# Value products of the second attention in split fp32r, heads in pairs, the residual kept in DRAM meanwhile

## What is computed

```python
h = rms_norm_2(x, norm_mix)
proj = h @ w_in                      # q, 3 pairs of k and v, gates, pool input, merge gates
a = nsa_attention(...) @ w_branch_attn
b = pool_mixer(u_pool, pool_w, pool_scale) @ w_branch_pool
ga, gb = jnp.split(jax.nn.sigmoid(g_merge), 2, axis=-1)
x = x + (ga * a + gb * b) @ w_out
h = rms_norm_2(x, norm_mlp)
return x + jnp.square(jax.nn.relu(h @ w_ff1)) @ w_ff2
```

```python
e = jnp.exp(s - jnp.max(s, axis=-1, keepdims=True)) * mask
p = e / jnp.maximum(jnp.sum(e, axis=-1, keepdims=True), 1e-30)
o = g[0] * o_cmp + g[1] * o_sel + g[2] * o_win
```

## Time and profile before

| | us |
|---|---|
| median of 3 runs | 1099.92 |
| lowest and highest run | 1099.74, 1104.56 |
| the profiled execution | 1103.73 |
| its span, first to last instruction | 1101.9 |

### The profile page before, as it was taken

The page is one execution under the profiler, slowest core; times in us unless marked ns, Lnnn a source line. Parts: engine busy times, 40 slices in busy tenths (PEclk is TensorE's granted clock), DMA queues, the critical chain, the costliest instruction groups (busy, mean ns, idle before and its releaser), DMA issues. The chain is left out here.

```text
span 1101.9 us, 14350 instructions
## 1 busy us (share of the span) xinstructions
PE 1078.1 (98%) x5666; PEld 889.8 (81%) x5666; DVE 562.1 (51%) x1076; ACT 449.4 (41%) x814; POOL 80.2 (7%) x90
## 2 busy tenths in 40 slices
PE   7999999999899999999999999999999999999997
PEld 5788877888788888878788888888888888888885
DVE  5578997666864236233666878352222223333334
ACT  7454345545542432353433543233333333222223
POOL 0022110003400007200000000000000000000000
PEclk9999999999999999998999999999999999999999
DMA  8554332125120473131100611243322232224002
GB/s 314 111 114 106 97 95 77 41 61 188 49 87 1 139 223 86 39 90 46 38 1 1 211 44 56 73 153 118 131 77 77 83 147 77 77 77 144 10 1 76
DMA packets 73649, 100.09 MB, mean 91 GB/s; under 512 B 3776, under 2 KB 41408, under 8 KB 73584
## 3 DMA queue, kind: packets, MB, share of 16 engines
q1 hardware_dynamic: 72800, 96.43, 27.1%
q0 software_dynamic: 784, 2.75, 1.7%
HBM read 96.42 MB, written 2.75 MB: 90 GB/s over the span
## 5 line engine op out<-in xcount | busy, mean ns | idle before, releaser
L2036 DVE TENSOR_TENSOR w_lo<-wring,w_hi 128x1024 fp32r<-128x1024 f32 x64 | 78.5, 1226 | 238.1 <-ACT w_hi L1524 238.1
L1524 ACT ACTIVATE w_hi<-wring 128x1024 fp32r<-128x1024 f32 x64 | 67.7, 1058 | 211.5 <-PE bank L736 211.5
L736 PE MATMUL bank<-u_hi,h_hi 128*128 128x512 f32 (+1 forms) x288 | 110.9, 385 | 1.0 <-ACT x L1227 0.8
L736 PE MATMUL bank<-u_hi,h_lo 128*128 128x512 f32 (+1 forms) x288 | 109.2, 379 | 0.0
L736 PE MATMUL bank<-u_lo,h_hi 128*128 128x512 f32 (+1 forms) x288 | 109.0, 378 | 0.0
L1609 DVE TENSOR_TENSOR u_lo<-wring,u_hi 128x1024 fp32r<-128x1024 f32 (+1 forms) x64 | 78.8, 1240 | 53.9 <-ACT u_hi L1309 53.3
L736 PE MATMUL bank<-h_hi,w_lo 128*128 128x512 f32 (+2 forms) x272 | 104.5, 384 | 0.0
L736 PE MATMUL bank<-h_hi,w_hi 128*128 128x512 f32 (+2 forms) x272 | 104.4, 384 | 0.0
L736 PE MATMUL bank<-h_lo,w_hi 128*128 128x512 f32 (+2 forms) x272 | 104.3, 384 | 0.0
L736 PE MATMUL bank<-w_lo,ff_hi 128*128 128x512 f32 x256 | 101.0, 395 | 0.0
L1309 ACT ACTIVATE u_hi<-wring 128x1024 fp32r<-128x1024 f32 (+1 forms) x64 | 65.7, 1032 | 86.0 <-PE bank L736 70.1
(11 more groups left out here) (285 smaller groups left out, 2030.0 us busy)
## 6 DMA issues: line engine op xcount, KB each, us to landing
wring<-in_w_ff SPq DMA_DIRECT2D x16, 2048.0 KB, 8.1
wring<-in_w_in SPq DMA_DIRECT2D x60, 512.0 KB, 3.9
arena<-in_w_out SPq DMA_DIRECT2D x4, 1024.0 KB, 5.0
wring<-in_w_out SPq DMA_DIRECT2D x2, 2048.0 KB, 13.2
arena<-in_first SPq DMA_DIRECT2D x8, 418.0 KB, 6.8
arena<-in_x SPq DMA_DIRECT2D x4, 512.0 KB, 10.6
arena<-bias_copies POOLq DMA_DIRECT2D x8, 256.0 KB, 6.3
arena<-bias_copies SPq DMA_DIRECT2D x32, 64.0 KB, 2.2
```

Source lines behind the costliest of these rows:

```text
L736: last = mm(b, lhs, rhs, start=(start and n == 0), stop=(stop and n == 2))
L1524: run(dst, src, ACT.Copy).then_inc(w_hi_done, 1)
L2036: v.tensor_tensor(cut(w_lo[ring3(m)]), src, cut(w_hi[ring3(m)]).bitcast(F32), ALU.subtract).then_inc(w_lo_done, 1)
```

## The change

The value products change roles. `v2_both` holds, for each branch, tile and group, 64 columns of high half and 64 of low half side by side, 128 weights wide. The moving operand is the transposed probabilities of two heads of one group, 256 columns, once as `pt_hi` and once as `pt_lo`. The result is the attention transposed, with the high half's rows 0 to 63 and the low half's 64 to 127 of a bank; ACT copies the low rows to SBUF (`low_rows`) and DVE adds them per head (`collect2`) into `attnT`, which is kept transposed.

Since the rows of the result are no longer the query rows, the scaling by gate over sum moves ahead of the transposes: DVE takes the reciprocal of two sums, and POOL multiplies each probability row by it and by the gate. Both branches then accumulate in one bank. `steps2` is ordered tile, head pair, branch, head. There are six `logits2` buffers, and transposes run two passes behind the scores, values three. ACT takes the high half of the transposed probabilities, DVE the low one.

The compression branch is scaled before its transposes too, and its four products give `attnT` at once. The attention transposes go. Branch products 0 and 1 move up behind the transposes of the last two pairs. The fills are spread over steps 0 to 52.

`v2_both` and the `pt` halves need room, part of which is where `x` lies: SP writes `x` to DRAM among the loads of the second block, and reads it back when the last value product is done.

```diff
-    steps2 = [(i, br, h) for i in range(NT) for br in ("s", "w") for h in range(NH)]
+    steps2 = [(i, br, 2 * m + r) for i in range(NT) for m in range(NH // 2) for br in ("s", "w") for r in range(2)]
...
-    fill2 = [(m, FILL2[m // KC], m % KC) for m in range(KC * len(FILL2))]
+    fill2 = [(m * 9 // 8, FILL2[m // KC], m % KC) for m in range(KC * len(FILL2))]
...
-    BRANCH_HIGH = {56: 0, 59: 1}
+    BRANCH_HIGH = {58: 0, 62: 1}
...
-    AT_STEP = {50: 0, 54: 1, 58: 2}
+    AT_STEP = {56: 0, 58: 1, 60: 2}
...
+                        if U2 + 5 <= u < U2 + 9:
+                            i = u - U2 - 5
+                            sp.wait_ge(xn_done, i + 1)
+                            sp.dma_start(x_kept[i], x[:, i, :]).then_inc(x_out, 16)
...
                 if name == "w2o1":
+                    sp.wait_ge(pv_done, 2 * NS)
+                    sp.wait_ge(x_out, 16 * NT)
+                    for i in range(NT):
+                        sp.dma_start(x[:, i, :], x_kept[i]).then_inc(x_back, 16)
                     for e in range(3, KC):
                         load_branch(e)
...
             def turn2(u):
-                pe.wait_ge(e_done, NS + u + 1)
+                pe.wait_ge(scaled, u + 1)
...
+            def value2(t):
+                i, br, h = steps2[t]
+                o, at, n = t // NH, t % NH // 4 * 256, t // 2 % 2
+                pe.wait_ge(t_free, TT[("pt", NS + t + 1)] + 1)
...
                 for j in range(i + 1):
+                    for part in (pt_hi, pt_lo):
+                        last = mm(bank[6 + o % 2][:, at:at + 256], v2_both[:, "sw".index(br), j, h // GROUP, :, :].rearrange("p m d -> p (m d)"),
+                                  part[n][:, 256 * j:256 * (j + 1)], start=(br == "s" and j == 0 and part is pt_hi),
+                                  stop=(br == "w" and j == i and part is pt_lo))
+                last.then_inc(pv_done, 2)
...
+            pe.wait_ge(v2_lo_done, 2)
+            for t in range(0, NS + 6, 2):
                 if t < NS:
                     pe.wait_ge(l_done, NS + t)
                     pair2(t)
                     fill(fill2, t)
                     fill(fill2, t + 1)
+                if 4 <= t < NS + 4:
+                    turn2(t - 4)
+                    turn2(t - 3)
+                if t >= 6:
+                    value2(t - 6)
+                if t == NS:
+                    pe.wait_ge(a_free, A2_END)
+                    pe.wait_ge(pm_lo_done, 4)
+                if t in (NS, NS + 2):
+                    branch_product((t - NS) // 2)
...
+            for t in range(0, NS + 8, 2):
+                if t < NS:
+                    exps(t, steps2, NS, den2, logits2)
+                if 4 <= t < NS + 4:
+                    prob_high(t - 4)
+                    prob_high(t - 3)
+                if t < NS:
+                    exps(t + 1, steps2, NS, den2, logits2)
+                if t >= 14 and t % NH == 6:
+                    low_rows((t - 14) // NH)
+                if t in AT_STEP:
+                    attn_high(AT_STEP[t])
...
             def collect2(o):
+                i, g = o // G2, o % G2
+                dve.wait_ge(lo_rows_done, o + 1)
...
+                for r in range(2):
+                    v.tensor_tensor(turned[r * HD:(r + 1) * HD, :].rearrange("p (m s) -> p m s", m=2), cut(bank[6 + o % 2][0:HD, :], r),
+                                    cut(lo_rows, r), ALU.add).then_inc((turned_done, o_free)[r], 1)
...
+                place = attnT[:, 2 * g:2 * g + 2, i * P:(i + 1) * P]
+                v.tensor_tensor(place, place, turned.rearrange("p (m s) -> p m s", m=2), ALU.add).then_inc(attn_done, 1)
...
+            for t in range(0, NS + 8, 2):
+                if t < NS:
+                    score2(t)
+                if 2 <= t < NS + 2:
+                    dve.wait_ge(e_done, NS + t)
+                    v.reciprocal(den2[:, t - 2:t], den2[:, t - 2:t]).then_inc(rden_done, 1)
+                if t < NS:
+                    score2(t + 1)
+                if 4 <= t < NS + 4:
+                    prob_low(t - 4)
+                    prob_low(t - 3)
+                if t >= 14 and t % NH == 6:
+                    collect2((t - 14) // NH)
                 if t - 2 in AT_STEP:
                     attn_low(AT_STEP[t - 2])
...
+            for u, (i, br, h) in enumerate(steps2):
+                if u % 2 == 0:
+                    pool.wait_ge(rden_done, u // 2 + 1)
+                place = logits2[u % 6][:, 0:(i + 1) * P]
+                at = (NH if br == "s" else 2 * NH) + h
+                g.tensor_scalar(place, place, den2[:, u:u + 1], gates[:, i, at:at + 1], ALU.mult, ALU.mult).then_inc(scaled, 1)
```

More of the change, by code:

```diff
@@ L252, in build @@
         x = sb("x", [P, NT, D])
+        x_at = nc.sbuf_base - 4 * NT * D
         hT_at = nc.sbuf_base
@@ L1103, in _ @@
-            for t in range(0, NS + 4, 2):
+                    for part in (pt_hi, pt_lo):
[3 more added lines that the diff above has]
+                last.then_inc(pv_done, 2)
+            R = 2 * NT
@@ new lines, in branch_product @@
+            def branch_product(at):
+                e, n = BRANCH[at]
+                pe.wait_ge(br_lo_done, e + 1)
+                if at >= 4:
+                    pe.wait_ge(r_free, 2 * NT + at - 3)
+                act = (a_hi, a_lo) if n == 0 else (pm_hi, pm_lo)
+                for k in range(4):
+                    last = three(bank[(2 * NT + at) % 4][:, :], (br_hi[e % 2], br_lo[e % 3]), slice((4 * n + k) * P, (4 * n + k + 1) * P),
+                                 act, slice(k * S, (k + 1) * S), True, k == 0, k == 3)
+                last.then_inc(r_full, 1)
@@ L1460, in _ @@
                         split_high(m)
+                    act.wait_ge(x_out, 16 * NT)
+                    for n, br in enumerate("sw"):
+                        act.wait_ge(a_free, AT[("kv2" if br == "s" else "kwvg", NT - 1)] + 1)
+                        run(v2_both[:, n, :, :, 0, :], v2[br].rearrange("p i (g d) -> p i g d", g=G2), ACT.Copy).then_inc(v2_hi_done, 1)
                 if kind == "hidk":
@@ new lines, in prob_high @@
+            def prob_high(u):
+                n, r = u // 2 % 2, u % 2
+                k = TT[("pt", NS + u)]
+                blocks = steps2[u][0] + 1
+                act.wait_ge(t_full, k + 1)
+                if u >= 4:
+                    act.wait_ge(pv_done, NS + 2 * (u // 2) - 2)
+                run(pt_hi[n][:, :].rearrange("p (j r s) -> p j r s", r=2, s=P)[:, 0:blocks, r, :],
+                    bank[4 + k % 2][:, 0:blocks * P].rearrange("p (j s) -> p j s", s=P), ACT.Copy).then_inc(pt_hi_done, 1)
@@ new lines, in low_rows @@
+            def low_rows(o):
+                act.wait_ge(pv_done, NS + NH * (o + 1))
+                if o >= 1:
+                    act.wait_ge(o_free, NS // NH + o)
+                run(lo_rows, bank[6 + o % 2][HD:P, :], ACT.Copy).then_inc(lo_rows_done, 1)
+            act.wait_ge(pooled, len(POOL_WINDOWS))
+            act.wait_ge(v2_lo_done, 2)
+            for t in range(0, NS + 8, 2):
[10 more added lines that the diff above has]
+                    attn_high(AT_STEP[t])
+                for u in (t, t + 1):
+                    takes(fill2, u)
+                    if u in GB_HIGH:
+                        high(GB_HIGH[u])
+                    if u in BRANCH_HIGH:
+                        branch_high(BRANCH_HIGH[u])
@@ L1953, in collect2, with prob_low @@
-            def collect2(o):
-                i = steps2[NH * o][0]
-                dve.wait_ge(o_free, NS // NH + o + 1)
-                ins = v.tensor_tensor(attn[:, i, :], attn[:, i, :], junk[:, 0:512], ALU.add)
-                if o % 2 == 0:
-                    step(ins)
-                else:
-                    ins.then_inc(attn_done, 1)
+            def prob_low(u):
+                n, r = u // 2 % 2, u % 2
+                k = TT[("pt", NS + u)]
+                blocks = steps2[u][0] + 1
+                part = lambda a: a[n][:, :].rearrange("p (j r s) -> p j r s", r=2, s=P)[:, 0:blocks, r, :]
+                dve.wait_ge(pt_hi_done, u + 1)
+                v.tensor_tensor(part(pt_lo), bank[4 + k % 2][:, 0:blocks * P].rearrange("p (j s) -> p j s", s=P),
+                                part(pt_hi).bitcast(F32), ALU.subtract).then_inc(t_free, 1)
@@ L1969, in _ @@
+                v.tensor_tensor(part(a_lo), attnT[:, :, i * P:(i + 1) * P], part(a_hi).bitcast(F32), ALU.subtract).then_inc(at_lo_done, 1)
+            for n, br in enumerate("sw"):
+                dve.wait_ge(v2_hi_done, n + 1)
+                v.tensor_tensor(v2_both[:, n, :, :, 1, :], v2[br].rearrange("p i (g d) -> p i g d", g=G2),
+                                v2_both[:, n, :, :, 0, :].bitcast(F32), ALU.subtract).then_inc(v2_lo_done, 1)
             dve.wait_ge(co_free, NT)
-            dve.wait_ge(pooled, len(POOL_WINDOWS))
```

178 lines of the change are left out of this document (60 added, 118 removed).

## The result

The changed kernel takes 1106.88 us (median of 20 runs, 1101.01 to 1110.31), the kernel before, in 20 runs beside it, 1101.84 (1099.46 to 1104.71): a ratio of 1.0034, with a 95% interval of 1.0017 to 1.005. The forecast was 1099.4, half a microsecond less than the 1099.92 that three runs had given for the kernel before (in twenty runs it is at 1101.84). So the change makes it slower, by about 4 us. The runs of the changed kernel lie in groups: six at 1101.0 to 1103.2 with a mean clock of 0.994, the others at 1104.3 to 1110.3 with 0.986 to 0.991. The profiled execution took 1106.16 with a span of 1104.4; its counterpart of before had 1101.9.

What follows compares the result with a forecast made beforehand. PE, busy 98% of the span, was taken as the bound. S moving from 648.0 to 647.2, plus 0.3 behind it, gave -0.5 on 1099.92: 1099.4 us, range 1088 to 1109.

Steps and rivals of the forecast that it cites:

- S: Start of the first branch product that reads the attention: 648.01 before, forecast 647.2; the change is worth its shift.
- (a): Rival: PE stays the bound to the end, DVE and ACT overlapping better; S 636.4, total 1088.6; chance 0.17.
- Value products: 160 fp32 blocks of 0.195 to 0.21 become 160 fp32r matmuls of 0.12: 32 us becomes 19 on PE.
- Head of the loop: Ahead of the second attention's loop: two more DVE subtractions, +1.2 us, start at 529.3.
- Laps 0 to 46: Second attention's loop passes, two heads each, before pair 48: 79.15 us becomes 67.9, other engines hidden while fill runs.
- Laps 48 to 60: Later loop passes: DVE and ACT chain takes 3.4 plus extras, sum 28.9 us, pair 62 ends at 627.0.
- Tail: From the end of pair 62 to S: 17.5 us, including 3.3 of PE idle.
- POOL: 64 new scalings in the loop at 1.5 us per 512 columns, lower bound 0.5, upper 3.0; fits barely.
- POOL against DVE: Six DVE operations with two SBUF operands before S each wait about 0.45 us: +2.7, bounds 0 and 6 x 1.5.
- Behind S: Dense PE work left alone; ACT's table load and sigmoids come ahead of branch 2's high half: +0.3 us.
- (c): Rival: the clock falls to half at PE's 3.3 us stall: at most +5, 1104.5; chance 0.18.
- (b): Rival: two-factor scaling costs POOL much more, p each, pacing row tile 3; S = 614.6 + 16p; chance 0.15.

Runs made afterwards that it cites:

- The last experiment: Changed kernel with value low half early, second branch product last, wide products among narrow ones, and DVE and ACT chain cut: 1092.07 us, ratio 0.991 to before.

## Why the prediction was wrong

**The time, point by point.** S was forecast at 647.2 and came at 647.7, but that is luck: the loop's start came 2.0 early, laps 0 to 46 took 4.4 more, from there to the end of pair 62 2.3 less, and the tail 0.4 more. The step that failed is the one behind S, "dense PE work that the change leaves alone": the clock, which I had priced as a rival, is the loss. (A small slip beside it: rival (a) prices the five chunks at 3.9, the sum for laps 0 to 46 at 3.5.)

- *Value products*: right. They start 0.12 apart in groups, with 0.20 behind the first.
- *Head of the loop*: right. The wait grew by 1.25 (2.03 against 0.78), 1.2 forecast. That the loop started at 527.30 and not 529.3 is the stretch of the earlier trace rows, 3.4 us long in this execution and 10.3 in that of before. What I had not asked is what the longer wait does: in this execution 3.2 us at half clock behind it, 1.6 lost.
- *Laps 0 to 46*: wrong by 4.4 (72.3 against 67.9). 1.6 are that stretch. 3.3 are waits for DVE ahead of pairs 18, 26 and 34 (1.49, 1.42, 0.40): the step "all hidden while fill runs" failed. I had weighed busy shares of DVE per lap and not its order: collecting four pairs, with its wait for ACT's low rows, stands ahead of the next scores, in every eighth step and not only in lap 54. Where a lap had one or two chunks of fill, 2 to 3 us long, that was too much; ahead of pair 26 DVE had a weight split of 1.22 (L1650 at 561.78) in its queue as well. PE idle in laps below 48 is what the forecast had itself named a sign of being wrong in kind. The last experiment, with the collecting placed where nobody waits, has none of these waits.
- *Laps 48 to 60*: right in the chain of laps 54 to 60, wrong by 2.3 over the whole. DVE's first scores of pairs 54 to 62 lie 5.2, 3.4, 4.0 and 5.0 apart (611.72, 616.90, 620.30, 624.25, 629.26); 5.1, 3.4, 4.0 and 5.2 were forecast. But pair 48 had started 2.4 late (599.57 against 597.2), and that pair 62 still ended at 627.1, forecast 627.0, is a coincidence: in laps 48 and 50 DVE took 3.0 and 3.2 instead of 3.9, and at the end PE ran ahead of the chain, for DVE came to the score of pair 62 only at 629.26.
- *Tail*: 20.6, forecast 17.5 and 2.7 of mutual waiting, 20.2: right in sum, wrong in its parts. I let DVE's last lap begin when PE's pair 62 ended; DVE began it at 629.26, 2.2 later, so PE waited 2.8 for the low halves of the pair before and did a value group and part of the first branch product at half clock. The 2.7 of mutual waiting did not come. That POOL's last two scalings took 1.5 and not 3.0 gave nothing: they were done at 636.8, and PE came for them at 638.50. The idle time ahead of S, 3.3 forecast, was 3.5.
- *POOL*: the step that took the one-factor row for the two-factor scaling, 1.5 with a lower bound of 0.5, failed in size: 0.77, half of the row. The Trainium skill (GPSIMD Engine Reference, section 4.1 Engine selection) calls one-input work on this engine "roughly line-rate"; for the two-factor form at 512 columns, 0.77 against DVE's 0.69, this case's trace nearly agrees, for the one-factor form, 1.56, it does not.
- *POOL against DVE*: of six operations one met POOL at work, the branch split at 636.29, 1.60 us against 1.22. With POOL done in half the time there is little to meet. The term was 2.7 and is 0.4.

```profile
L1655 DVE TENSOR_TENSOR br_lo<-wring,br_hi x8: 1216/1218/1596, 628.1 to 679.9; 128x1024 fp32r<-128x1024 f32 x8
```

- *DMA*: right, nothing. The residual's transfers land in 5.1 us, and no matmul waits for them.
- *Behind S*: wrong, the term that decides. "Everything from S on is dense PE work that the change leaves alone" was true of the work and not of the clock. With the clock up, S to the end took 454.0 in five traces, 0.1 more than before (0.3 forecast); with the wait of 3.50 ahead it took up to 456.7, 2.8 more.

**The rivals.** (c) was what happened. Its bound, "at most +5" for the one place, held (2.8 behind S); wrong were its chance, 0.18, and its place, one stall: a mechanism that I allowed for at the stall of 3.3 had to be asked of every wait of over a microsecond, and the runs lose 5.6 us more to the clock than before. The argument against it, that no idle time of 3 us lay in the attention, was lack of evidence, read as evidence. And the trace of the kernel before had rows that I had not used, at its very start, where PE first waits 6.53 us:

```profile
6.53 0.77 PE L736 MATMUL bank<-h_hi,first_hi 128*128 128x512 f32 x1 [6.53 <-DVE h_lo L1651]
7.09 0.63 PE L736 MATMUL bank<-h_lo,first_hi 128*128 128x512 f32 x1
7.52 0.63 PE L736 MATMUL bank<-h_hi,first_lo 128*128 128x512 f32 x1
...
12.15 0.39 PE L736 MATMUL bank<-h_lo,first_hi 128*128 128x512 f32 x1
12.38 0.40 PE L736 MATMUL bank<-h_hi,first_lo 128*128 128x512 f32 x1
```

Up to 11.8 these matmuls start 0.43 apart, as the first ones behind S in the changed kernel do (648.31, 648.74, 649.17), and from 12.15 on 0.23 apart. The clock column reads 1.00 there, so only the spacing shows it, and it is the start of the program, not a wait in its midst; but it was a reason to give (c) more than 0.18. (b) is far away at a price of 0.77, and (a) needed a DVE queue without the collecting and the a_lo steps ahead of the scores; the last experiment is nearly that case, at S = 636.5.

The median lay within the range of 1088 to 1109, three of the twenty runs above it.

**What stays open**: how long a wait must be. Counted over the traces kept, from the loop's head to S:

| wait of PE, us | where | waits | clock fell |
|---|---|---|---|
| 3.50, 3.71 | ahead of S, once ahead of a branch product | 7 | 7 |
| 2.63 to 2.83 | behind lap 62 | 7 | 5 |
| 2.03 | head of the loop | 7 | 3 |
| 1.84 to 2.11 | laps and behind lap 62 (high halves first, fill spread) | 5 | 5 |
| 1.69, 1.76 | behind lap 62, ahead of a branch product (fill spread) | 2 | 0 |
| 1.53, 1.54 | ahead of pair 58 | 6 | 5 |
| 1.41 to 1.52 | ahead of pairs 18 and 26 | 14 | 0 |

(The waits for POOL in the run with two scalings are left out.) So among the waits from 1.5 to 2.8 us the length alone does not decide it. Open is also why the stretch of the earlier trace rows is 3.4, 6.8 or 10.3 us long in kernels that are the same up to there.

## What to carry to other kernels

When a change takes work from an engine that was always busy, ask of each wait that appears not only how long it is but what the clock does behind it: a wait of 3.5 us cost up to 2.8 more behind it, and useful work moved into it gave that back and part of the wait. Lay out every engine's queue for the laps with extra steps, not for the mean lap, and put such a step where nobody waits for what is behind it. A price taken from another form of an instruction is a bound in neither direction.

## What the runs showed of the hardware

- POOL multiplies by two factors in less than half the time that it needs for one: 0.65 against 1.50 us at 496 columns, with nothing changed in it but a second factor of 1.0; 0.77 against 1.56 to 1.65 at 512.
- A two-factor scaling takes 0.55 at 128 columns and 0.77 at 512, so most of it does not depend on the width.
- The clock fell to 0.50, mostly for 3.4 or 6.8 us, at each of seven waits of 3.5 to 3.7 us and at some of those of 1.5 to 2.8 us, and did not fall ahead of S when that wait was filled with products that nobody reads. The stretch behind the 32-column products, where PE was busy all the time, went as well when wide products stood among them.
- A 64-row product of 32 columns and a 128-row one of 512 next to each other cost: three wide products among the narrow ones take 0.28 us more than apart, for the change to the wide ones and back.
